# Splitting each weight chunk in one instruction per engine in place of two halves

## What is computed

```python
def memory_kv(mem_n, w_kv, k_gain):
    mk, mv = split_cols(mem_n @ w_kv, [MEM_WIDTH, MEM_WIDTH])   # 256 tokens x 1024 -> 2 x 512
    mk = rmsnorm(mk.reshape(bsz, nm, MEM_HEADS, MEM_HEAD_DIM), k_gain)
    ...

def mlstm_layer(x, ...):
    qk, v, o, z, i_pre, f_pre, mq, mz = split_cols(rmsnorm(x, norm_g) @ w_in, [...])
    ...
    return x + jnp.concatenate([y_m, y_mem], axis=-1) @ w_out

def second_block(x, mem, ...):
    ...
    proj = rms_norm(x, g_mix[l]) @ w_in[l]
    ...
    x = x + mixed @ w_out[l]
    x = x + memory_cross_attention(rms_norm(x, g_cross[l]), rms_norm(mem, g_mem[l]), w_cq[l], w_ckv[l], w_co[l])
    x = x + jnp.square(jax.nn.relu(rms_norm(x, g_mlp[l]) @ w_up[l])) @ w_down[l]
    return rms_norm(x, g_final)
```

## Time and profile before

| | us |
|---|---|
| runs (three) | 1577.17, 1579.07, 1579.16 |
| median | 1579.07 |
| the profiled execution, its own time | 1579.46 |
| its span in the trace | 1577.7 |
| TensorE busy / standing still | 1531.7 / about 39 in 32 pauses, 8.0 of them at the start |
| VectorE / ScalarE / GpSimd busy | 890.2 / 715.3 / 223.5 |

### The profile page before, as it was taken

One profiled execution on the slowest core, in us unless ns is written; L12 is line 12 of the kernel. 1 busy time (PEld: TensorE's weight loads), 2 busy tenths in 40 slices (PEclk: granted clock), 3 DMA queues, 4 the chain that ended last, 5 costly groups with the idle time before them and its releaser, 6 DMA issues.

```text
span 1577.7 us, 19176 instructions
## 1 busy us (share of the span) xinstructions
PE 1531.7 (97%) x7086; PEld 1239.6 (79%) x7086; DVE 890.2 (56%) x1753; ACT 715.3 (45%) x1630; POOL 223.5 (14%) x194
## 2 busy tenths in 40 slices
PE   7998999999999999999899999999999999999998
PEld 5886777877898777777587878788777888888886
DVE  6467485657565566666457557664455444434344
ACT  6553343334355667665335354442344433324243
POOL 3203020202120003122022005220001100000001
PEclk9999999999999999999999999999999999999999
DMA  6522121323424221112133312134323333333332
GB/s 194 161 68 80 54 80 55 107 68 120 119 76 147 77 61 56 54 56 67 41 121 94 94 55 67 56 109 131 93 81 94 94 93 96 105 94 93 97 103 81
DMA packets 88636, 141.56 MB, mean 90 GB/s; under 512 B 6368, under 2 KB 36448, under 8 KB 88544
## 3 DMA queue, kind: packets, MB, share of 16 engines
q1 hardware_dynamic: 87824, 139.55, 29.3%
q10 hardware_dynamic: 720, 0.80, 0.2%
HBM read 138.23 MB, written 2.10 MB: 89 GB/s over the span
## 4 chain that ended last, share of the span: by engine, by line
PE 79%; DVE 8%; ACT 5%; issue 3%; POOL 3%; DMA 2%; SPq 0%; ACTq 0%; POOLq 0%; DVEq 0%
PE banks L1259 12%; PE banks L1261 12%; PE banks L1260 12%; PE banks L1264 10%; PE banks L1266 10%; PE banks L1265 10%; PE banks L1222 3%; DVE sb_w_split L1964 3%; ACT sb_junk L1529 2%; DVE sb_arena L1973 2%; PE banks L1437 1%; PE banks L1384 1%; ACT sb_w_split L1561 1%; PE banks L1500 1%; DVE sb_arena L1964 1%
## 5 line engine op out<-in xcount | busy, mean ns | idle before, releaser
L1964 DVE TENSOR_TENSOR sb_w_split<-sb_raw,sb_w_split 128x512 fp32r<-128x512 f32 (+4 forms) x530 | 345.0, 693 | 365.9 <-ACT sb_w_split L1561 365.5
L1561 ACT ACTIVATE sb_w_split<-sb_raw 128x512 fp32r<-128x512 f32 (+4 forms) x530 | 288.1, 592 | 411.2 <-PE banks L1261 192.0
L1259 PE MATMUL banks<-sb_actA,sb_w_split 128*128 128x512 f32 x672 | 277.1, 412 | 2.8 <-DVE sb_arena L1964 2.5
L1261 PE MATMUL banks<-sb_actA,sb_w_split 128*128 128x512 f32 x672 | 263.0, 391 | 0.0
L1260 PE MATMUL banks<-sb_actA,sb_w_split 128*128 128x512 f32 x672 | 262.1, 390 | 0.0
L1264 PE MATMUL banks<-sb_w_split,sb_actB 128*128 128x512 f32 (+2 forms) x464 | 181.4, 391 | 1.6 <-DVE sb_w_split L1964 1.6
L1266 PE MATMUL banks<-sb_w_split,sb_actB 128*128 128x512 f32 (+2 forms) x464 | 175.9, 379 | 0.0
L1265 PE MATMUL banks<-sb_w_split,sb_actB 128*128 128x512 f32 (+2 forms) x464 | 175.5, 378 | 0.0
L1264 PE MATMUL banks<-sb_w_split,sb_actA 128*128 128x512 f32 (+1 forms) x384 | 154.4, 402 | 13.5 <-DVE sb_w_split L1964 9.6
L1259 PEld LDWEIGHTS banks<-sb_actA,sb_w_split 128*128 128x128 f32 x672 | 126.5, 188 | 32.7 <-issue 7.1
L1266 PE MATMUL banks<-sb_w_split,sb_actA 128*128 128x512 f32 (+1 forms) x384 | 150.3, 391 | 0.0
(11 more groups left out here) (226 smaller groups left out, 2188.2 us busy)
## 6 DMA issues: line engine op xcount, KB each, us to landing
sb_raw<-in_a_w_in SPq DMA_DIRECT2D x66, 256.0 KB, 3.0
sb_raw<-in_w_up SPq DMA_DIRECT2D x32, 512.0 KB, 3.8
sb_raw<-in_w_down SPq DMA_DIRECT2D x32, 512.0 KB, 3.8
sb_raw<-in_w_in SPq DMA_DIRECT2D x24, 512.0 KB, 3.7
sb_raw<-in_mem_w_kv SPq DMA_DIRECT2D x16, 512.0 KB, 3.8
sb_raw<-in_w_ckv SPq DMA_DIRECT2D x16, 512.0 KB, 3.8
sb_raw<-in_a_w_in SPq DMA_DIRECT2D x15, 512.0 KB, 3.7
sb_raw<-in_a_w_out SPq DMA_DIRECT2D x12, 512.0 KB, 3.9
```

Of the source, the lines that this page charges most:

```text
L1259: pe.op.matmul(out, hi[:, cs], x.hi(k), start=i == 0, stop=False)
L1261: t = pe.op.matmul(out, lo[:, cs], x.hi(k), start=False, stop=last_i)
L1561: act.op.activation(hi[:, cs], raw[:, cs], ACT.Copy).then_inc(act.mark(m("w_hi"), 2 * n + part + 1), 1)
L1964: dve.op.tensor_tensor(out, a, b, op).then_inc(dve.mark(*mark) if mark else dve.tick(), 1)
```

## The change

Each chunk's rounding becomes one ScalarE instruction over the whole chunk, and its remainder one VectorE instruction over the whole. The semaphores `w_hi` and `w_lo` are raised by two at once, so every other wait keeps its number. VectorE's wait is for the whole rounding. The 530 roundings become 265, and so do the subtractions. No other step, buffer or transfer is changed, and nothing changes places in any engine's list. The lines below move up by three on ScalarE's side and by six on VectorE's; the subtraction of a split is recorded at its own line, L2015, the rounding at L1558.

```diff
@@ -1555,10 +1555,7 @@
             act.wait_ge(m(f"dma_raw{n % RAW_SLOTS}"), m.raw_total(n))
             if n >= SPLIT_SLOTS:
                 act.wait_ge(*m.chunk_done(n - SPLIT_SLOTS))
-            half = raw.shape[-1] // 2
-            for part in range(2):
-                cs = slice(part * half, (part + 1) * half)
-                act.op.activation(hi[:, cs], raw[:, cs], ACT.Copy).then_inc(act.mark(m("w_hi"), 2 * n + part + 1), 1)
+            act.op.activation(hi, raw, ACT.Copy).then_inc(act.mark(m("w_hi"), 2 * n + 2), 2)
@@ -2014,11 +2011,8 @@
             n = a[0]
             name, c = plan.chunks[n]
             raw, hi, lo, _ = v.chunk(n, name, c)
-            half = raw.shape[-1] // 2
-            for part in range(2):
-                cs = slice(part * half, (part + 1) * half)
-                dve.wait_ge(m("w_hi"), 2 * n + part + 1)
-                tensor(lo[:, cs], raw[:, cs], hi[:, cs].bitcast(F32), ALU.subtract, m("w_lo"), 2 * n + part + 1)
+            dve.wait_ge(m("w_hi"), 2 * n + 2)
+            dve.op.tensor_tensor(lo, raw, hi.bitcast(F32), ALU.subtract).then_inc(dve.mark(m("w_lo"), 2 * n + 2), 2)
```

## The result

The changed kernel is slower: 1587.36 us median of five runs (1583.36 to 1588.14) against 1577.17 (1573.44 to 1579.16) of the kernel before on the same chip, a ratio of 1.0064 (95% interval 1.0048 to 1.0081). Measured twice more, in company with the experiments, it was 1.0045 (1.0032 to 1.0058) and 1.0040 (1.0024 to 1.0056). So the loss is 6 to 10 us, where 3.6 were forecast, and the median of the first measurement lies 1.1 us above the range; the two later ones, with medians 6.0 and 6.4 us above before, lie in it. Three of all the executions ran at a granted clock of 0.66 to 0.85 and took 1708 to 2196 us; no ratio or mean here contains them. The profiled execution took 1587.13 us, its span 1585.3: 7.6 us more than before.

The account below looks back on a forecast made before the run. TensorE bounds the kernel (busy 1531.7 of 1577.7 us); ScalarE and VectorE count only where it waits. Terms 0.95 + 0.90 + 1.75 + 0.50 + 0.80 - 0.13 - 1.15 = +3.6 us on the 1579.07 median gave 1582.7; range 1579.0 to 1586.3.

Parts of the forecast that it names:

- The unit: A full chunk: ready 2.31 us after ScalarE's start instead of 1.95, 0.35 us later wherever VectorE waits for ScalarE.
- Memory products: Two products at 36 to 60 us: three raw-buffer turns each 0.35 us longer, +1.05 at most, +0.95 taken.
- Softmax rounds: Seven of fourteen softmax waits have a split right before them: +0.25 us each, +1.75; lower bound 0.7, upper 2.45.
- the slack of the next: Softmax rounds: one round's shift is partly absorbed by the next, one reason for charging +0.25 us each, not 0.35.
- The cross attention: Two splits in series at projection w_cq, +0.70 us, and a like chain at 1055 to 1063 us, +0.20: sum +0.90.
- The two splits at 487 and 502 us: Two splits before an eviction, where TensorE waits 0.35 us or has no slack: +0.25 each, +0.50 us.
- The gains: Fewer or shorter blockings with GpSimd: -0.75 us from 135 us on, -0.30 at 235.5, -0.10 at 611; sum -1.15.
- The start: First wait, 8.0 us, gets +0.14; short waits at 16.9 and 38.9 us give back 0.27; sum -0.13.
- absorbed: Rival: shifts at softmax rounds and memory products vanish in later slack; +1 us, so 1580; chance 0.27.
- it doesn't do what it says: Rival: one 1024-column ScalarE instruction takes more than two of 512, so chunks come later still; no chance of its own.
- Fewer turns: Rival: whole chunks meet GpSimd's lock less often, at three or four places on the path; -2 us, about 1577; chance 0.07.
- Slower still: Rival: memory-product and GpSimd-blocking terms doubled, softmax term at 2.45; +7 us, so 1586; chance 0.16.

Follow-up runs that it names:

- e11_wait_both: Kernel before, with halves on both engines, but VectorE waits for both roundings before its first half; 1588.85 against 1576.83 us, ratio 1.0068.
- e2_stream: Kernel before with whole chunks only from chunk 193 on (cross attention's output projection and MLP); 1577.64 us, ratio 1.0002.
- e8_whole_heads: Kernel before with whole chunks only in chunks 25 to 41, halves elsewhere raising semaphores by two; 1577.84 us, ratio 1.0000.
- e3_act_whole: Kernel before with only ScalarE's rounding whole; VectorE subtracts in two halves, both behind the whole rounding; 1582.06 us, ratio 1.0034.
- e7_rounds: Kernel before with whole chunks only in chunks 89 to 136 (latent attention with its softmax rounds); 1576.05 us, ratio 0.9997.
- e13_second: Kernel before with whole chunks in chunks 137 to 264 (from 811 us), halves ahead; 1581.10 us, ratio 1.0027.
- e1_cross: Kernel before with whole chunks only in chunks 157 to 192 (about 944 to 1157 us); 1579.94 against 1577.07 us, ratio 1.0017.
- e5_quarters: Kernel before with four quarters on each engine in place of two halves; 1585.57 us, ratio 1.0056.

## Why the prediction was wrong

The direction, the mechanism and most of the places were right: a chunk that is ready later where VectorE waits for ScalarE, hidden in the streams, not hidden in the memory products, the softmax rounds and the cross attention. e11_wait_both shows the mechanism by itself, e2_stream the cover. The size was wrong. TensorE stands still 4.6 to 5.6 us longer in the three profiles of the changed kernel, where the sum of the terms was 3.6, and the clock came on top. By its own terms:

1. *The unit.* The forecast was 1.05 + 0.04 + 1.22 = 2.31 us; it is 1.06 + 0.10 + 1.23 = 2.39. The 0.04 held for subtractions that raise their semaphore by one; the change raises it by two, and VectorE goes 0.07 us later (e8_whole_heads has this with halves, e3_act_whole lacks it behind a whole rounding). That is 0.08 more at some dozen places, 1 us in all by this estimate, and not a price of merging as such.
2. *Memory products.* +1.1 to +1.3 for +0.95: three turns of 0.43 are 1.3. The mechanism held; the bound of 1.05 was too low by the unit.
3. *Softmax rounds.* The forecast was +1.75, and -0.10 at 611; TensorE fell behind by 1.9 to 2.0 from 520 to 771 us in all three profiles (the jumps behind 771 are the low clock, 3.4 or 6.8 us of it). Seven pauses grew by 0.31 to 0.43, 2.7 in all, where seven times 0.25 was charged: "the slack of the next" did not take its share. Others shrank, by 0.37 at 548 us, which the forecast didn't see, and by 0.10 at 611 us, which it did. So the term came out nearly right by two errors against each other.
4. *The cross attention: the step that failed most.* The pause at 1063 was charged +0.20 for "its end is shared with other work", and it grew by 0.7 in TensorE's wait and 0.8 to 0.9 in all. In both traces its chain is the same: VectorE's work on the row, a split that VectorE starts late, the transfer it releases, a second split, and VectorE's last step. Nothing else shares the end. The second split is ready 0.47 us later on it, and 0.23 is lost ahead of an earlier split, where VectorE stands idle and the trace names no releaser. The pause at 997 was charged nothing and grew by 0.56 (TensorE's delay by 0.87), through GpSimd. The projection w_cq at 1098, +0.70, has its two splits in series as forecast, but the transfer between them took 4.33, 3.73 and 3.85 us in the three profiles where it had taken 4.25, so only the first shows the term (+0.76; +0.15 and +0.25 in the others). The two splits at 487 and 502 us, +0.50, gave +0.1 to +0.4.
5. *TensorE's clock* isn't in the forecast at all. A pause on the one critical place grew by 0.7 us and cost another 1.5, and one that shrank by 0.4 gave back another 1.7. These two nearly cancel, but the mean granted clock of the changed kernel was lower than before in both later measurements (0.9924 for 0.9939, 0.9937 for 0.9944), which by the rate of the last section is 1.4 and 0.7 us. With the pauses of the profiles, 4.6 and 5.6 us, this gives 6.0 and 6.3, for 6.0 and 6.4 measured. Both are estimates from one profile each. For the first measurement, five runs of each kernel, the clocks of the kernel before aren't on record; with those of the later ones the same estimate gives 7 to 8 us, so 2 to 3 of its 10.2 stay unexplained.
6. *The gains.* Forecast -1.15. (Its own items for 142, -0.9, twice -0.07 and +0.35, make -0.69 rather than -0.75.) The pause at 142 became 0.45 shorter, not the 0.9 less of one turn behind GpSimd. In the changed kernel's timeline the two chunks there are one undisturbed subtraction and one that still stood behind a product of GpSimd, for the earlier trace rows:

```profile
136.93 1.22 DVE L2015 TENSOR_TENSOR sb_w_split<-sb_raw,sb_w_split 128x1024 fp32r<-128x1024 f32 x1
...
137.36 1.74 POOL L2599 TENSOR_TENSOR sb_arena<-sb_arena 128x512 f32<-128x512 f32 x1 [3.31 <-ACT sb_arena L1741]
...
138.33 1.85 DVE L2015 TENSOR_TENSOR sb_w_split<-sb_raw,sb_w_split 128x1024 fp32r<-128x1024 f32 x1 [0.18 <-ACT sb_w_split L1558]
...
139.18 1.96 POOL L2601 TENSOR_TENSOR sb_arena<-sb_arena 128x512 f32<-128x512 f32 x1
...
140.30 0.99 DVE L1964 TENSOR_SCALAR sb_arena<-sb_arena,sb_small 128x256 f32<-128x256 f32 x1
...
143.86 0.77 PE L1264 MATMUL banks<-sb_w_split,sb_actA 128*128 128x512 f32 x1 [3.02 <-DVE sb_arena L1970]
```

From 136.93 to 138.33 + 1.85 = 140.18 the two take 3.25 us for 4.29: 1.04 us saved, more than the 0.9 forecast. But GpSimd's products took 1.74 and 1.96 us in place of 1.40 and 1.42, and VectorE's next long step on the chain, the scaling of 256 columns, now stood beside the second of them: 0.99 us, where the kernel before has 0.35 at 139.40. So 0.64 of the gain went back to a turn behind GpSimd, at another instruction of the same engine.
7. *The start* was forecast with +0.14 and lost 0.4 to 0.6 in two profiles of the changed kernel; but in profiles with halves there it varies from -0.1 to +0.6 as well (e7_rounds, e13_second), so the profiles can't tell the change's share. The 0.27 given back at 16.9 and 38.9 didn't come.

Of the rivals, "absorbed" is out (the three measurements, and e1_cross with 2.9 us in one stretch), and so is "it doesn't do what it says": the 1024-column rounding is 1.06 us. "Fewer turns" names a true mechanism, 1.79 us for 2.32 at 630 us, which is outweighed. "Slower still" came nearest in time, 1586, with half of the right reason: its GpSimd term at more places is there, but the stretches with late fetches that it doubled were those of the cross attention. Its sum is partly luck: by its stated terms (3.62 + 0.95 + 0.80 + 0.70) it is +6.1, which gives 1585.1, not +7. The rule of the Trainium skill ("Perfetto Trace Analysis", "Optimizing Scalar/DVE Operations") that breaking up instructions may let work be completed sooner where the engine isn't saturated is borne out by e11_wait_both; its limit is shown by e5_quarters, where quarters were ready earlier and the kernel lost 7.5 us. That page weighs the one against the other by saturation; here the engines are half busy on average and the loss comes in stretches in which VectorE and GpSimd work side by side.

## What to carry to other kernels

Two engines that pass a buffer on in parts are a pipeline, and merging the parts cost up to one part's duration at each hand-over here (0.36 us for a part of 0.62), even though it saved instructions: look at who waits on whom first, and count only the places where the next engine stands waiting for the whole. To find those places, take every pause of the engine that sets the time and follow its chain back through all hand-overs, transfers and GpSimd included; each hand-over on the chain counts once more. When parts are merged, look also at what the merged instruction raises: here a raise by two made each hand-over 0.07 us later. Where a change makes a pause longer, price the clock behind the pause as a term of its own, and measure in many runs: one profile of this kernel can be 5 us from the next.
